# Wider column groups and 256-column products in a two-layer transformer forward pass

## The reference

```
for l in 0, 1:
    shift, scale, gate (two sets) = silu(c) @ w_mod[l] + b_mod[l]          # 2048 x 12288
    ux = rmsnorm(x) * gain * (1 + scale) + shift
    l = 0: f, q, k, v = ux @ att_w_in   (1024 + 1024 + 256 + 256 columns); k, v of the context too
           mix = concat(fft2(f).real, attention(rope(q), rope(k), v, sink)) @ att_w_out
    l = 1: gb, gc, xv = split(ux @ conv_w_in)  (3 x 2048 columns)
           mix = (gb * conv3(gc * xv)) @ conv_w_out
    x = x + gate * rmsnorm(mix) * gain
    x = x + gate' * rmsnorm(relu(modulate(x) @ w1)**2 @ w2) * gain'         # w1 2048 x 8192, w2 8192 x 2048
```

## Time and profile before

| | |
|---|---|
| Three runs | 2500.5, 2502.68, 2503.95 us; median 2502.68 us |
| Profiled execution | span 2501.8 us from first to last instruction; its mean granted clock is 0.958 |
| Busy | PE 2287.4 us, weight loads 1941.8 us, DVE 1880.4 us, ACT 1136.6 us, POOL 209.2 us |
| Transfers | 583.02 MB, a mean of 233 GB/s |

### The profile page before, as it was taken

One profiled execution on the slowest core, in us unless ns is written; L12 is line 12 of the kernel. 1 busy time (PEld: TensorE's weight loads), 2 busy tenths in 40 slices (PEclk: granted clock), 3 DMA queues, 4 the chain that ended last, 5 costly groups with the idle time before them and its releaser, 6 DMA issues.

```text
span 2501.8 us, 37308 instructions
## 1 busy us (share of the span) xinstructions
PE 2287.4 (91%) x12351; PEld 1941.8 (78%) x12351; DVE 1880.4 (75%) x1848; ACT 1136.6 (45%) x1407; POOL 209.2 (8%) x64
## 2 busy tenths in 40 slices
PE   6888866969999999999987999996999999999997
PEld 5666744858888888888876878885888888888886
DVE  5678787678878878878878987787886755655665
ACT  5664434545444444444454334444544444444454
POOL 0001023020101101100101100012010100000000
PEclk8999988979999999999998999998999999999998
DMA  8878766747887888888765877775788565655553
GB/s 291 275 244 264 240 193 211 248 155 252 263 286 260 270 280 269 270 266 284 242 229 166 294 265 257 245 259 177 236 270 275 178 192 185 185 187 185 184 190 101
DMA packets 433781, 583.02 MB, mean 233 GB/s; under 512 B 17827, under 2 KB 382899, under 8 KB 433203
## 3 DMA queue, kind: packets, MB, share of 16 engines
q1 hardware_dynamic: 433714, 582.24, 71.2%
HBM read 580.07 MB, written 2.10 MB: 233 GB/s over the span
## 4 chain that ended last, share of the span: by engine, by line
PE 67%; DVE 16%; issue 6%; DMA 6%; ACT 3%; POOL 1%; DVEq 1%; SPq 0%; ACTq 0%; POOLq 0%
PE ps L455 42%; PE ps L457 21%; DVE acc L990 5%; DVE wlo L970 4%; DMA mraw<-in_w_mod_dram 3%; DMA raw<-in_w_mod_dram 2%; PE ps L479 2%; ACT whi L637 1%; PE ps L481 1%; POOL red L1461 1%; DVE t L1003 1%; POOL red L1465 1%; DVE fq L1332 1%; PE ps L436 1%; DVE fq L1129 1%
## 5 line engine op out<-in xcount | busy, mean ns | idle before, releaser
L970 DVE TENSOR_TENSOR wlo<-raw,whi 128x1024 fp32r<-128x1024 f32 x776 | 979.4, 1281 | 418.5 <-ACT whi L637 403.3
L637 ACT ACTIVATE whi<-raw 128x1024 fp32r<-128x1024 f32 x776 | 807.6, 1056 | 791.0 <-PE ps L457 611.7
L455 PE MATMUL ps<-u,whi 128*128 128x512 f32 x3136 | 1116.6, 400 | 32.6 <-DVE wlo L970 28.4
L457 PE MATMUL ps<-u,wlo 128*128 128x256 f32 x3136 | 881.8, 281 | 0.0
L455 PE MATMUL ps<-h,whi 128*128 128x512 f32 x2368 | 842.6, 399 | 16.4 <-DVE wlo L970 11.9
L455 PEld LDWEIGHTS ps<-u,whi 128*128 128x128 f32 x3136 | 592.2, 189 | 184.2 <-DVE wlo L970 35.7
L457 PE MATMUL ps<-h,wlo 128*128 128x256 f32 x2368 | 666.0, 281 | 0.0
L457 PEld LDWEIGHTS ps<-u,wlo 128*128 128x128 f32 x3136 | 595.4, 190 | 0.0
L455 PEld LDWEIGHTS ps<-h,whi 128*128 128x128 f32 x2368 | 448.1, 189 | 127.0 <-DVE wlo L970 13.2
L457 PEld LDWEIGHTS ps<-h,wlo 128*128 128x128 f32 x2368 | 450.3, 190 | 0.0
L990 DVE SCALAR_TENSOR_TENSOR acc<-mraw,cs,acc 128x1024 f32<-128x1024 f32 x278 | 366.3, 1317 | 19.7 <-DMA mraw<-in_w_mod_dram 17.8
(11 more groups left out here) (130 smaller groups left out, 1130.8 us busy)
## 6 DMA issues: line engine op xcount, KB each, us to landing
raw<-in_mlp_w_dram SPq DMA_DIRECT2D x512, 512.0 KB, 4.3
mraw<-in_w_mod_dram SPq DMA_DIRECT2D x278, 512.0 KB, 5.4
raw<-in_w_mod_dram SPq DMA_DIRECT2D x106, 512.0 KB, 4.9
raw<-in_conv_w_in_dram SPq DMA_DIRECT2D x96, 512.0 KB, 5.8
raw<-in_att_w_in_dram SPq DMA_DIRECT2D x40, 512.0 KB, 5.7
raw<-in_att_w_out_dram SPq DMA_DIRECT2D x32, 512.0 KB, 4.7
raw<-in_conv_w_out_dram SPq DMA_DIRECT2D x32, 512.0 KB, 5.2
fq<-in_x_dram SPq DMA_DIRECT2D x1, 2048.0 KB, 10.8
```

What stands on the lines that cost most here:

```text
L455: pe.matmul(ps[:, bk, :], whi[:, s, c * GW + m * P:c * GW + (m + 1) * P], inp[:, k, :], start=(k == 0), stop=False)
L457: last = pe.matmul(ps[:, bk, 0:T], wlo[:, s, c * GW + m * P:c * GW + (m + 1) * P], inp[:, k, 0:T], start=False, stop=(k == KC - 1))
L637: act.activation(whi[:, s, :], raw[:, s, :], ACT.Copy).then_inc(hi_ready, 1)
L970: dve.tensor_tensor(wlo[:, s, :], raw[:, s, :], whi[:, s, :], ALU.subtract).then_inc(lo_ready, 1)
```

## The change

1. A group has 512 output columns, 8 slabs of 2 chunks each (`GW = 512`, `CPS = 2`, `SL = 8`). A slab is as large as before, but its rows in memory are 2 KB long where they were 1 KB. There are half as many groups.
2. A weight tile takes three matmuls of 256 columns, which all add into the same 256 PSUM columns. A bank holds two finished tiles, and a group fills two banks. Nothing is left to be added: `tmp`, line 748 and `add_halves` go.
3. Groups turn through four pairs of banks (three in the convolution). A group's first bank is announced (`half_done`) once its part of the last slab is done. Results are taken out while the next group's fourth slab is converted (`step`), the two halves one after the other: `h` from a relu on ACT and a multiply on DVE that reads PSUM, `y` by a DVE add, the squares of the output projections by ACT from PSUM, `fin`, `kT`, `vsum` and `cgc` by ACT copies, the rope's cosine by DVE from PSUM.
4. The inner loops over groups are written out; the loop over quarters remains (1 to 3 on DVE, ACT and SP, 1 to 4 on PE). In the convolution nothing is looped.
5. In the last group before a boundary DVE and ACT convert three slabs of the next stage, and all of the unit's slabs come before `finish_unit` and the squares. The boundary then converts one slab instead of four.
6. `UNIT_SHARE` goes from ten groups to five: (2,3,3,3,4,4,4,3,8,4) to (4,6,7,7,14), 38 in both. K and V are one group.

```diff
-GW = 256
+GW = 512
 SLOTS = 4
-CPS = KC // SLOTS
+CPS = 2
+SL = KC // CPS
+UNIT_AT = ((0,), (1,), (), (), (), (2,), (3,), ())
+UNIT_CLOSING = ((0,), (1,), (2, 3))
...
-                                pe.matmul(ps[:, bk, :], whi[:, s, c * GW + m * P:c * GW + (m + 1) * P], inp[:, k, :],
-                                          start=(k == 0), stop=False)
-                                last = pe.matmul(ps[:, bk, 0:T], wlo[:, s, c * GW + m * P:c * GW + (m + 1) * P],
-                                                 inp[:, k, 0:T], start=False, stop=(k == KC - 1))
+                    for half in range(2):
+                        for c in range(CPS):
+                            k = s * CPS + c
+                            for m in range(2):
+                                col = c * GW + (2 * half + m) * P
+                                hi_w = whi[:, s % SLOTS, col:col + P]
+                                lo_w = wlo[:, s % SLOTS, col:col + P]
+                                for i, inp in enumerate((src,) if src2 is None else (src, src2)):
+                                    o = ps[:, pairs[i][half], m * T:(m + 1) * T]
+                                    pe.matmul(o, hi_w, inp[:, k, 0:T], start=(k == 0 and m == 0), stop=False)
+                                    pe.matmul(o, hi_w, inp[:, k, T:2 * T], start=False, stop=False)
+                                    last = pe.matmul(o, lo_w, inp[:, k, 0:T], start=False,
+                                                     stop=(k == KC - 1 and m == 1))
+                        if s == SL - 1 and half == 0:
+                            last.then_inc(half_done, 1)
...
-                act.activation(tmp[:, :, :], ps[:, bank:bank + 2, T:2 * T], ACT.Copy).then_inc(b_copied, 1)
...
-                dve.tensor_tensor(dst, ps[:, bank:bank + 2, 0:T], tmp[:, :, :], ALU.add).then_inc(sum_done, 1)
...
+            def step(w, units, take=None, after=None, closing=False):
+                for s in range(3 if closing else SL):
+                    if s == 3 and take:
+                        take()
+                    lo(w + s, s % SLOTS)
+                    units(s)
+                    if s == 3 and after:
+                        after()
+                if closing:
+                    if take:
+                        take()
+                    if after:
+                        after()
...
+                def last():
+                    finish_unit(last_unit, unit_col(last_unit))
+                    squares(3)()
+                step(w_ahead, stage_units(un, 4, 3, un % 2, UNIT_CLOSING), None, last, closing=True)
...
-                los(w0)
+                lo(w0 + 3, 3)
...
-UNIT_SHARE = (2, 3, 3, 3, 4, 4, 4, 3, 8, 4)
+UNIT_SHARE = (4, 6, 7, 7, 14)
```

More of the change, by code:

```diff
@@ L568, in _ @@
             pe.wait_ge(o_ready, HEADS)
-            stage_groups(PG_WO, 8, u, lambda s: [])
+            for i in range(4):
+                group(PG_WO + i, u, (pair_of(i),))
             def boundary_sums(j, n_sq):
@@ L778, in _, with rope_swaps @@
[L778 to L803 removed]
+            def rope_swaps(r, pair):
+                for half in range(2):
+                    rope_swap(r + half, pair[half])
@@ L913, in mlp, with relu_of, f @@
-                with act.Fori(0, 2) as q:
-                    quarter(q + 1, lambda pg, i: None)
-                stage(pg0, 8, h_high(3), 3)
+                pg0, n0 = PG_MLP[l], 32 * l
+                def relu_of(q, i):
+                    def f():
+                        for half in range(2):
+                            n = q * 8 + (n0 + 2 * i + half)
+                            if half == 0:
+                                act.wait_ge(half_done, q * 8 + (pg0 + i + 1))
+                            else:
+                                act.wait_ge(slab_used, q * 64 + slab_of(pg0 + i + 1))
+                            if not (isinstance(n, int) and n < 2):
+                                act.wait_ge(relu2_ready, n - 1)
+                            act.activation(relu1[half], two_tiles(pair_of(i)[half]), ACT.Relu).then_inc(relu1_ready, 1)
+                    return f
@@ L1351, in quarter, with take_h, f @@
-                def quarter(q, un, n_m, col, take2, first=False):
-                    stage(pg0, 8, un, n_m, take_h(q), q, 0, first)
+                pg0, n0 = PG_MLP[l], 32 * l
+                def take_h(q, i):
+                    def f():
+                        for half in range(2):
+                            n = q * 8 + (n0 + 2 * i + half)
+                            dve.wait_ge(relu1_ready, n + 1)
+                            if not (isinstance(n, int) and n < 2):
+                                dve.wait_ge(h_ready, n - 1)
+                            dve.scalar_tensor_tensor(out=relu2[half], in0=two_tiles(pair_of(i)[half]), scalar=0.0,
+                                                     in1=relu1[half], op0=ALU.max, op1=ALU.mult).then_inc(relu2_ready, 1)
+                    return f
@@ L1363, in take_last, with squares, f @@
-                def take_last(pg, bank, i):
-                    add_to_y(3)(pg, bank, i)
-                    add_squares(i + (8 + 16 * l), 1 + 2 * l)
-                stage(pg0, 8, u0 + 6, loop_units, take_h(3), 3, 0)
+                quarter(0, u0, 4, unit_col(u0), first=True)
+                with dve.Fori(1, 3) as q:
+                    quarter(q, q * 2 + u0, loop_units, q * KC + (unit_col(8) - KC))
+                def squares(i):
+                    def f():
+                        for half in range(2):
+                            add_squares(8 + 16 * l + 2 * i + half, half)
+                    return f
```

812 lines of the change are left out of this document (381 added, 431 removed).

## The result

| | before | after |
|---|---|---|
| median of the runs (us) | 2501.59 (2490.89 to 2503.95, 4 runs) | 2548.18 (2545.33 to 2552.97, 4 runs) |
| profiled span (us) | 2501.8 | 2551.2 |
| tile of the products, mean in a stream (us) | 0.3515 | 0.3600 |

The change makes the kernel slower: ratio 1.0209, 95% interval 1.0168 to 1.0249. 2488 was forecast; the time came out where the first rival had put it (2546). The `before` column is the three runs of the kernel before and a fourth one. In the later rounds single executions of the kernel before lie anywhere from 2479.9 to 2508.6 us, and its profiled one (span 2501.8) is in the upper half; so the ratios, each taken within one round, say what a kernel is worth, and the spans say where the time went.

A forecast was written before the change was run, and what follows sets the result against it. PE was taken as the bound, with 2022 of 2502 us in streamed tiles. Terms -6 - 12 - 2 - 11 - 8 + 17 + 4 + 3 = -15 gave 2487, forecast 2488 us; own range 2462 to 2508, 8-in-10 range 2440 to 2540.

The forecast's parts named there:

- the first rival: All 5760 weight tiles: the third matmul has a price of its own; at 0.36 us a tile 2546 us; chance 0.20.
- The products: All 5760 weight tiles: three 256-column matmuls take 0.350 us against 0.351, so -6 us; rounding bounds -121 and +52.
- the third rival: PE's stops remain and the input projection's end pays +25: 2528 us, or 2515 with half the stops; chance 0.18.
- The stops when GpSimd starts: PE's waits for wlo mostly go: -12 first MLP, -2 second, -11 convolution and output projection, -8 input projection; bounds 0, -42.
- The end of the input projection: Behind the last wlo DVE has 15 unit slabs instead of 6 ahead of the keys' rope: +17 us, bounds +3.5 and +25.
- The boundaries: Three boundaries and the end: unit slabs and finish_unit ahead of the squares, three wlo fewer; +4 us, bounds -12 and +15.
- Loops: PE's jump back over eight written-out groups per quarter may leave it without instructions: +3 us, bounds 0 and +12.
- Evictions and transfers: 180 ACT copies and as many DVE adds go, and rows become 2 KB moving the same bytes: both worth 0.

The follow-up runs named there:

- e1: Kernel before with its 512-column matmul cut into two of 256 columns, each with its own columns; ratio 1.0156, span 2532.2 us.
- e3: Changed kernel with the first product 384 columns wide (512 for a group's first chunk), part of the products left out; 2263.81 us, one run.
- e8: Changed kernel with PE's loop over the three later quarters of an MLP written out; ratio 1.0146 to the kernel before, span 2526.0 us.
- e2: Changed kernel with the first product 512 columns wide again, mixing two tiles' sums; ratio 0.9892 to the kernel before, span 2472.8 us.
- e5: Kernel before with each chunk's matmuls reordered, both 512-column ones first, then both 256-column ones; ratio 0.9985, span 2484.2 us.
- g2: Kernel before with finish_unit moved from between stages to behind the second slab of the next stage's first pair; 2481.2 us, ratio 0.9947.
- e7: Changed kernel with finish_unit behind the squares in the last group before each boundary; ratio 1.0152 to the kernel before, span 2531.3 us.

## Why the prediction was wrong

**The products: the step that failed.** "I stay by the mean, since 0.24 is just two of 0.12: the trace shows no start-up that a matmul pays once whatever its width." -6 was taken, +49 measured, close to the upper bound of +52. The mistake has two parts. Three intervals behind the 256-column matmul (0.1167 each) were added up to a tile without a 512-column one, though the trace could show the sum of the two kinds only. The recorded starts split that sum in proportion to the columns; the tiles of e1 and e3 ask for a split of 226.7 and 120.0. An interval between two different instructions carries the difference of how their starts are recorded, and this cancels only over a whole period. And in the stretch of the earlier trace rows a tile takes 0.3533, one of the two values of before, so the nine intervals there spoke for that stretch alone; with 0.120, within the rounding of the earlier trace rows, the sum is 0.360. The first rival had the right mechanism and 0.36, with a chance of 0.20. (In the third rival 2515 takes off half of 25 us of stops; half of the 33 that had been taken would make it 2512.)

The quoted rule of the Trainium skill ("TensorE: Matmul & The Clock Gate", Back-to-back issue gap) has the right form, columns / 2.4 ns plus something fixed, and was set aside because of the split of the starts. Its 2.5 ns would be +14 us; the runs show 13.3 ns with these weights. The section gives the 2.5 ns as the gap of a matmul by itself and says that in a stream with weight loads between the matmuls both set the spacing; here a weight tile is loaded for every matmul, also when it is the one just used (2465 loads to 2466 matmuls in after's window of 300 us). The prediction applied the rule without that condition.

**The stops when GpSimd starts.** Right in kind, low in size: -33 was taken in all, about -54 came, beyond the bound of -42. The input projection gave -1.5 instead of -8 (its waits for `wlo` are 11.0 for 12.3), the first MLP -24 for -12, the convolution and its output -24 for -11, the second MLP -4 for -2. The step that failed is the price of a stop: it was taken as PE's wait alone, and the time at the granted clock of 0.50 behind it (13.6 us in the first MLP, 17.0 in the convolution) was put at nothing. In the convolution the waits of the earlier trace rows that were put down to transfers went too.

**The end of the input projection.** +17 was taken; the first mask on DVE comes 19.1 us later (329.92 for 310.84), and from PE's last product to the end of its wait it is +15.6. So the mechanism and the size are right. The core behind it is 7 us longer, which no step had. 2 of them are the scores that before ran ahead of the wait and after run behind it, since K and V are one group now. In the rest (from the first transposes on) the executions of the kernels built on before take 122.5 to 125.5 us, those built on after 124.5 to 127.5, and the profiled one of before is the shortest of all. So no more than 1 to 2 us on the mean are the change's; their cause is open.

**The boundaries.** +4 was taken, about +12 came (+13.4 for the three and -1.8 at the end), within the bound of +15. The adds stalled as expected: in the first boundary they end 10.3 us behind PE's last product for 3.0 before (+7.2, taken as +6.4). What failed are the subtractions. "2.9 us of it are paid in either order": the scaling of `y` does run without that stall now, but GpSimd's mask meets a later scaling of the same update (3.38 us for 1.21), so the whole update of `x` is 0.7 us shorter, not 2.9. And the three `wlo` give 2.4 instead of 3.5 up to the second root, and behind that root PE's first product comes 1.1 us later. Together that is the +5.3 of this boundary.

**Loops.** +3 taken, +21 measured by e8's stages, over the bound of +12: 14 in the gaps between starts, which were 2.8 to 4.0 us, and the rest in the lower clock behind them. The comparison with the jumps over two groups in the earlier trace rows misled. e2 narrows it: its body has the same eight groups with 1024 matmuls and stops for 0.5 to 0.8 us, that of after has 1536 and stops for 2.6 to 3.7.

**Evictions and transfers** at 0 stand as far as the accounts go: no stage shows a gain that the stops don't explain, and all that isn't tiles sums up to nothing.

Without the products the terms sum to nothing where -9 had been taken: the stops came 21 us better, the loops 18, the boundaries 8 and the way from the last product of the input projection through the core 6 worse. That these nearly cancel is luck; the products' 55 us were left alone.

## What to carry to other kernels

Count matmuls as well as columns: in the streams of 256, and of 384 and 256, columns a matmul with a 128 x 128 weight tile cost its columns / 2.4 ns and 13.3 ns more, so a split at equal columns is paid per tile; streams of 512 and 256 were at that sum in 27% of the stretches and 6.7 ns a tile above it in the others, so here the split cost 6.7 to 13.3 ns. Price a stop of TensorE with the slower clock behind it: 15.8 us of waiting came to 24. Take the price of an instruction in a pipeline from the period of a whole pattern, never from one interval between two unlike records. A read that releases GpSimd goes where the engine it stalls has slabs in hand, and never between the last product and the sums that the next stage waits for.

## What the runs showed of the hardware

- The price per matmul follows the width of its weight tile: 13.3 ns at 128 columns, 6.7 ns at 64 (tiles of 0.360 and 0.340 us).
- A stream of matmuls of 512 and 256 columns in turn runs at 346.7 or at 353.3 ns a pair (27% and 73% of the stretches in before, 57% and 43% in e2), with one value nearly always held from one stop of TensorE to the next. In the order 512, 512, 256, 256 (e5) it runs at 348.3.
- Behind eight stops of TensorE in the first MLP and the convolution of before (2.2 to 6.2 us) the granted clock was 0.50 for 3.4 or 6.8 us (a tile 0.64 us); behind one of 2.2 us in the second MLP it stayed at 1.00.
- A jump back over eight written-out groups of 1536 matmuls leaves 2.8 to 4.0 us between two starts; over the same groups with 1024 matmuls it is 0.8 to 1.1 us, and with the quarters written out there is no gap. The queue of instruction fetches moved 151 packets in after, 106 in e2, 143 in e8 and 30 in before, so it is not their number.
- GpSimd's sum over the partitions (6.13 us) holds up a DVE instruction that reads two tensors from SBUF until about 4.4 us after the sum's start, and then that takes its usual time (5.62 for 1.41 in after; 6.68 for 2.35 in g2); the hold is shorter than the sum. It did not hold the reciprocal of one tensor beside it (1.75 us in e7, as always), nor, in the second boundary of after, the adds that read one of their two tensors from PSUM (L1336, 1.28 us for two across GpSimd's start).
